# Delta net with an order of its own for each engine and the last join's products in turn; S5 kernel products in four column groups

## The reference, cut to what matters

```python
# gated DeltaNet: 4 heads x 128, forward and backward, chunked
decay = jnp.where(tril, jnp.exp(jnp.where(tril, diff, 0.0)), 0.0)
a_mat = jnp.where(strict, jnp.einsum('bhnid,bhnjd->bhnij', kb, k) * decay, 0.0)
sys = jnp.eye(DN_CHUNK, dtype=q.dtype) + a_mat
sol = lax.linalg.triangular_solve(sys, rhs, left_side=True, lower=True, unit_diagonal=True)
attn = jnp.where(tril, jnp.einsum('bhnid,bhnjd->bhnij', q, k) * decay, 0.0)
def step(state, inp):
    v_new = u_i - jnp.einsum('bhck,bhkv->bhcv', w_i, state)
    o_i = jnp.einsum('bhck,bhkv->bhcv', q_i, state) + jnp.einsum('bhij,bhjv->bhiv', attn_i, v_new)
    state = state * jnp.exp(gl_i)[..., None, None] + jnp.einsum('bhck,bhcv->bhkv', k_i, v_new)

# S5: 32 groups x 16 channels, one 64-dim complex diagonal state per group, forward and backward
bu = jnp.einsum('blgp,gnp->blgn', u.astype(jnp.complex64), b_bar)
_, state = lax.associative_scan(_ssm_combine, (a, bu), reverse=reverse, axis=1)
y = jnp.real(jnp.einsum('blgn,gpn->blgp', state, c))
```

## Time and profile before

| | |
|---|---|
| median of 3 runs | 1445.17 us (1445.14 to 1446.3) |
| the profiled execution, its own time | 1445.08 us |
| its span in the trace | 1443.3 us, 24501 instructions |
| TensorE (PE) busy | 1324.0 us, 92% |
| VectorE (DVE) busy | 1055.1 us, 73% |
| ScalarE (ACT) busy | 859.0 us, 60% |
| GpSimd (POOL) busy | 377.0 us, 26% |
| `in_projection` | 0 to about 316 us |
| `delta_net` | about 318 to 526 us |
| the rest (S5, output projection, router, experts) | about 529 to 1443 us |

### The profile page before, as it was taken

How to read it: one execution, slowest core, us unless ns; L and a number is a source line. 1 busy time by engine, 2 the same in 40 slices (tenths; PEclk the granted TensorE clock), 3 DMA queues, 4 the chain that set the end, 5 groups by cost and what they waited for, 6 DMA issues and landing times. The chain is left out here.

```text
span 1443.3 us, 24501 instructions
## 1 busy us (share of the span) xinstructions
PE 1324.0 (92%) x8394; PEld 1116.5 (77%) x8394; DVE 1055.1 (73%) x1330; ACT 859.0 (60%) x1162; POOL 377.0 (26%) x377
## 2 busy tenths in 40 slices
PE   4999999977999879999973899999999999999994
PEld 3999888866888878668863688888888888888871
DVE  6895787674777648542127788888888888888847
ACT  7473435564656354562222588877788888777742
POOL 5020122008565637312201111111111111111130
PEclk9999999998999999999975899999999999999997
DMA  9174986411233129801114899999999999999865
GB/s 267 57 231 129 293 253 178 138 41 51 47 126 94 26 103 349 313 16 44 45 62 159 329 387 419 410 415 409 415 411 411 412 408 416 404 417 412 362 231 220
DMA packets 151607, 357.47 MB, mean 248 GB/s; under 512 B 42447, under 2 KB 97003, under 8 KB 124395
## 3 DMA queue, kind: packets, MB, share of 16 engines
q1 hardware_dynamic: 131755, 297.04, 54.8%
q0 software_dynamic: 11904, 40.42, 8.3%
q10 hardware_dynamic: 7872, 19.01, 3.3%
HBM read 287.64 MB, written 68.78 MB: 247 GB/s over the span
## 5 line engine op out<-in xcount | busy, mean ns | idle before, releaser
L2820 PE MATMUL gate_up_mm<-w_hi,gathered_T_hi 128*128 128x512 f32 x528 | 212.9, 403 | 7.8 <-DVE gathered_T_lo L3003 7.8
L2822 PE MATMUL gate_up_mm<-w_hi,gathered_T_lo 128*128 128x512 f32 x528 | 208.0, 394 | 0.0
L2821 PE MATMUL gate_up_mm<-w_lo,gathered_T_hi 128*128 128x512 f32 x528 | 207.5, 393 | 0.0
L2998 DVE TENSOR_TENSOR w_lo<-w_down,w_hi 128x2048 fp32r<-128x2048 f32 x66 | 148.5, 2289 | 51.9 <-ACT w_hi L2926 51.9
L2998 DVE TENSOR_TENSOR w_lo<-w_gate,w_hi 128x2048 fp32r<-128x2048 f32 x66 | 150.8, 2289 | 20.6 <-ACT w_hi L2926 19.7
L2926 ACT ACTIVATE w_hi<-w_gate 128x2048 fp32r<-128x2048 f32 x66 | 126.9, 1923 | 54.0 <-PE gate_up_mm L2822 32.2
L2926 ACT ACTIVATE w_hi<-w_up 128x2048 fp32r<-128x2048 f32 x66 | 126.7, 1922 | 49.9 <-PE down_mm L2857 49.9
L2998 DVE TENSOR_TENSOR w_lo<-w_up,w_hi 128x2048 fp32r<-128x2048 f32 x66 | 150.8, 2287 | 4.4
L2926 ACT ACTIVATE w_hi<-w_down 128x2048 fp32r<-128x2048 f32 x66 | 125.0, 1918 | 37.5 <-issue 17.9
L2771 POOL COPY gather_idx<-slot_token 128x1 int32 (+1 forms) x34 | 21.8, 640 | 477.1 <-PE x_turned L2810 450.3
L2820 PEld LDWEIGHTS gate_up_mm<-w_hi,gathered_T_hi 128*128 128x128 f32 x528 | 100.7, 191 | 33.6 <-issue 11.4
(11 more groups left out here) (506 smaller groups left out, 3063.2 us busy)
## 6 DMA issues: line engine op xcount, KB each, us to landing
w_down<-in_expert_w_down SPq DMA_DIRECT2D x66, 1024.0 KB, 7.2
w_gate<-in_expert_w_gate SPq DMA_DIRECT2D x64, 1024.0 KB, 7.5
w_up<-in_expert_w_up SPq DMA_DIRECT2D x64, 1024.0 KB, 8.3
expert_rows_dram<-ones SPq DMA_DIRECT2D x32, 512.0 KB, 6.3
expert_rows_dram<-expert_out ACTq DMA_DIRECT2D x32, 512.0 KB, 8.6
x<-s_rows_dram SPq DMA_DIRECT2D x9, 1184.0 KB, 6.9
s_rows<-s_rows_dram SPq DMA_DIRECT2D x7, 1184.0 KB, 8.1
w_raw<-in_w_in SPq DMA_DIRECT2D x12, 512.0 KB, 5.4
```

The source lines that it names most:

```text
L2820: pe.matmul(dst, xT_hi[:, k, :], hi[:, at, cols], start=k == 0, stop=False)
L2821: pe.matmul(dst, xT_hi[:, k, :], lo[:, at, cols], start=False, stop=False)
L2822: mm = pe.matmul(dst, xT_lo[:, k, :], hi[:, at, cols], start=False, stop=k == KT - 1)
L2998: dve.tensor_tensor(lo[:, at, :], flat(j), hi[:, at, :].bitcast(F32), ALU.subtract).then_inc(S["piece_lo"], 1)
```

## The change

Three parts.

1. `delta_schedule` takes the engine's name and yields from a table `STEP_ORDER` with a row for each of PE, DVE, ACT and GpSimd; an entry names operation, direction and chunk. So one engine's order no longer follows another's. ACT's `vdec` becomes an operation of its own: it reads `vnew` from SBUF, not V from PSUM, and PE waits for it before `new_state`, no longer before `attend`.
2. `z6` and `d6` are one entry for both directions, and their products alternate head by head between forward and backward.
3. The S5 kernel's 8 pairs of a call go to four groups of 32 output columns (partitions 0 to 127), in turn, and 2 pairs to each. The copies of ACT and DVE cover 128 partitions and a quarter of the columns. `store_M` issues 64 DMAs of a quarter of the size for each half, where there were 16.

```diff
+STEP_ORDER = {
+    "PE": "z4 f 0, z4 b 0, read_k f -1, read_k b -1, d4 f 0, d4 b 0, read_q f -1, read_q b -1, turn4 f 0, turn4 b 0, "
+          "solve f -1, solve b -1, z5 f 0, z5 b 0, attend f -1, attend b -1, d5 f 0, d5 b 0, kq f 1, kq b 1, "
+          "turn5 f 0, turn5 b 0, new_state f -1, new_state b -1, z6 f 0, kk f 2, kk b 2, d6 f 0",
+    "DVE": "read_k f -1, d4 f 0, read_k b -1, d4 b 0, base f 1, attend f -1, attend b -1, d5 f 0, d5 b 0, kq f 1, "
+           "kq b 1, new_state f -1, new_state b -1, kk f 2, kk b 2",
+    "ACT": "z4 f 0, z4 b 0, read_q f -1, turn4 f 0, turn4 b 0, solve f -1, solve b -1, z5 f 0, z5 b 0, read_q b -1, "
+           "vdec f -1, vdec b -1, turn5 f 0, turn5 b 0, decay f 2, z6 f 0, z6 b 0, decay b 2, d6 f 0, d6 b 0",
...
+}
-    steps = [("decay", 0), ("kk", 0), ("decay", 1), ("spread_tt", 0), ("alev4", 0), ("spread_t", 0), ("alev5", 0),
-             ("mask", 0), ("kk", 1), ("kq", 0)]
     for t in range(TT + 1):
-        steps += [("z4", t), ("alev4", t + 1), ("read_k", t - 1), ("vb", t), ("d4", t), ("base", t + 1),
-                  ("turn4", t), ("read_q", t - 1), ("z5", t), ("solve", t - 1), ("decay", t + 2), ("d5", t),
-                  ("attend", t - 1), ("mask", t + 1), ("alev5", t + 1), ("turn5", t), ("add_o", t - 1),
-                  ("new_state", t - 1), ("z6", t), ("kk", t + 2), ("kq", t + 1), ("d6", t),
-                  ("spread_tt", t + 1), ("spread_t", t + 1)]
...
                 elif name == "z6":
-                    wait("t_out", d, 2 * t + 2)
-                    wait("amat", d, t + 1)
-                    lo, up = late(d), early(d)
+                    for way in range(2):
+                        wait("t_out", way, 2 * t + 2)
+                        wait("amat", way, t + 1)
                     for h in range(H):
-                        mm = pe.matmul(X[d][up, h, 0:64], ab_b[d][lo, b, h, up], tt_b[d][lo, b, h, lo],
-                                       start=True, stop=True)
-                    mm.then_inc(S["z"][d], 1)
+                        for way in range(2):
+                            lo, up = late(way), early(way)
+                            mm = pe.matmul(X[way][up, h, 0:64], ab_b[way][lo, b, h, up], tt_b[way][lo, b, h, lo],
+                                           start=True, stop=True)
+                            if h == H - 1:
+                                mm.then_inc(S["z"][way], 1)
...
                 elif name == "attend":
-                    wait("vdec", d, t + 1)
                     wait("vn", d, t + 1)
...
                 elif name == "new_state":
+                    wait("vdec", d, t + 1)
                     wait("o_part", d, t + 1)
...
+                elif name == "vdec":
+                    wait("vn", d, t + 1)
                     wait("kv", d, t)
                     for h in range(H):
-                        ins = act.activation(vd_b[d][:, 0, h, :], V[d][:, h, :], ACT.Copy,
+                        ins = act.activation(vd_b[d][:, 0, h, :], vn_b[d][:, 0, h, :], ACT.Copy,
                                              scale=head_col("kdec", t, d, h))
...
             for t in range(T5):
-                for h in range(2):
-                    dst = self.dram[self.HJ * hf:self.HJ * (hf + 1), t * GC:(t + 1) * GC,
+                for ch in range(8):
+                    c, h = ch // 2, ch % 2
+                    dst = self.dram[self.HJ * hf + c:self.HJ * (hf + 1):4, t * GC:(t + 1) * GC,
                                     S5_M + P * h:S5_M + P * (h + 1)].rearrange("j p n -> p j n")
...
-        for j in range(self.HJ):
+        for x in range(2):
             for ri in range(2):
-                mm = pe.matmul(self.kps[:, j * P:(j + 1) * P], self.BD[:, ri, j, :],
-                               self.g_pair(u)[ri][:, j, d:d + T5, :].rearrange("p k q -> p (k q)"),
-                               start=ri == 0, stop=ri == 1)
+                for n in range(4):
+                    j = 4 * x + n
+                    mm = pe.matmul(self.kps[2 * GC * n:2 * GC * (n + 1), x * P:(x + 1) * P], self.BD[:, ri, j, :],
+                                   self.g_pair(u)[ri][:, j, d:d + T5, :].rearrange("p k q -> p (k q)"),
+                                   start=ri == 0, stop=ri == 1)
```

More of the change, by code:

```diff
@@ L1241, in _ @@
                 dve.memset(tt_b[d][:], 0.0).then_inc(S["cleared"][d], 1)
-            for name, t, d in delta_schedule():
+            for name, t, d in delta_schedule("DVE"):
                 ch, b = chunk(t, d), t % 2
@@ L1311, in _ @@
             act.activation(tmp_b[0][:, 0, 0, 0:1], c["ones"][:, 0:1], ACT.Exp)
-            for name, t, d in delta_schedule():
+            for name, t, d in delta_schedule("ACT"):
                 b, up = t % 2, early(d)
@@ L1380, in expand @@
                 return pool.tensor_tensor(dst[d][:, 0].rearrange("p h (b c) -> p h b c", c=16), cells, mask, ALU.mult)
-            for name, t, d in delta_schedule():
+            for name, t, d in delta_schedule("POOL"):
                 ch = chunk(t, d)
```

62 lines of the change are left out of this document (35 added, 27 removed), and 2 rows, old and new, of the table STEP_ORDER.

## The result

The changed kernel took 1438.19 us, median of five runs (1436.63 to 1439.3), against 1445.81 for the kernel before (1445.14 to 1449.26): ratio 0.9937, 95% interval 0.9926 to 0.9949. It is faster by 7.6 us where 20.2 were forecast, and the time lies outside the range. The profiled execution took 1439.3 us, its span 1437.6. A later series on another chip gave 0.9945 (0.9929 to 0.9961).

What follows compares the result with a forecast made beforehand. The prediction took PE to bound both the projection and `delta_net`, with DVE close behind in the latter. 9.0 us from the S5 products plus 11.2 from `delta_net` gave 20.2 off 1445.08: 1424.9 us, range 1418.0 to 1432.0.

Steps and rivals of the forecast that it cites:

- the walk through a steady step: PE and DVE in a `delta_net` step, operation by operation: the new step takes 22.7 us against 23.57.
- the wait before `kq`: In each steady `delta_net` step PE newly waits 1.6 us for DVE, whose `o` behind `base` frees bank V.
- the 0.6 us taken off for DVE: In the projection, 0.6 us off the 9.6 saved by four calls, as later savings meet DVE without idle time.
- S5 products: Four `multiply` calls on PE in the projection fall from 3.61 to 1.2 us each: 9.0 us saved in all.
- The rival of two groups: In the S5 calls at most two column groups overlap: 6.2 us saved instead of 9, 1427.7 us; chance 0.25.
- The pairs: `z6` and `d6` in `delta_net`, both directions in turn, take 0.54 us each: 0.82 us saved per step.
- So the saving of the pairs passes through: In `delta_net` the 0.82 us per step from `z6` and `d6` shortens the step, PE bounding it.
- the 2.6 us of step 4: The `delta_net` step of 25.19 us saves 2.6, as ACT's `decay` now stands behind the `turn5` copies.
- DVE binds the step: Rival: late blocks delay `base`, the wait before `kq` is 2.6 us, six steps save nothing: 1430.9 us; chance 0.13.
- step 0: First step of `delta_net`: saves its pairs and the wait before `turn4`, 0.82 + 1.26 = 2.1 us.
- the tail: End of `delta_net`: pairs, `turn4` wait and the last `attend`'s wait for `vdec` save 0.82 + 1.0 + 1.1 = 2.9 us.
- GpSimd's queue: Rival: `store_M`'s small DMAs cost c us each; from c = 0.86 the 20 us are gone, at 1.0 1465; chance 0.02.

Runs made afterwards that it cites:

- pairs_only: The kernel before with only `z6` and `d6` taking both directions in turn, all old orders kept: ratio 1.0004 to the kernel before.
- pairs_turn5: pairs_only with ACT's copies of `turn5` moved ahead of `decay`: ratio 0.9943 to the kernel before.
- mask_late: middle_early with GpSimd's masks held back until DVE's `base` is done: ratio 0.9895 to the kernel before.
- filled11: middle_early with 11 products of the identity before each `kq` f from the second step on: ratio 0.9941 to the kernel before.
- middle_early: The changed kernel with DVE's two additions of the first `kernel_middle` moved from j = 1 to the end of j = 0: ratio 0.9941 to the kernel before.

## Why the prediction was right or wrong

The step that failed is the walk through a steady step, in its term for the wait before `kq`: 1.6 us in the sum, 2.57 measured, because the new order puts GpSimd's masks beside DVE's `base` and the two hold each other up. With it came a cost that the sum did not have at all, the slower clock behind that wait. A second, smaller failure lies in the S5 part, in the 0.6 us taken off for DVE.

**S5 products, 9.0 us forecast, 6.0 as built.** The call: 1.2 forecast, 1.0 measured. The rival of two groups had 2.06 us to come out and is refuted: two records on the same columns don't hold up the neighbour's first. `store_M` cost 65.1 us / 128 = 0.51 a DMA (0.5 forecast) and nobody waited for it. What failed is "I take off 0.6" for DVE. The earlier trace rows showed idle time of DVE ahead of j = 2; I took it for room, but the third call needs what DVE does behind the convolution, a reduction and a weight split of j = 1. There DVE was only 3.4 us early, in a row without idle time, and the two faster calls before it take 5.2. So PE arrives first, and the wait of 2.3 to 2.7 us with the slower clock behind it takes back 2.6 us (8.6 with the repair, 6.0 without).

**The pairs, 0.82 a step.** They gave 0.68, at 0.61 us each where I said 0.54. "So the saving of the pairs passes through" was argued from PE's busy row. It is false in the old order: pairs_only gives nothing, for ACT's copy of `turn5` b was just in time. It passes only with ACT's new order, a part of the change on which my sum put no more than the 2.6 us of step 4. That step was right (25.19 to 22.72 in pairs_turn5).

**The wait before `kq`, 1.6 forecast, 2.57 measured.** This is the term that was mis-sized. The place, the releaser and the reason (`o` behind `base` on bank V) were right, and so was the walk: with the masks behind `base` the wait is 1.57 and the step 22.60, against 1.6 and 22.7, as long as `base` isn't late. What I left out is POOL's place in it: I took `base`'s 7.2 us from a step in which POOL was idle, and did not look at what POOL does beside it in the new order. The rival *DVE binds the step* had 2.6 us and 23.57 to come out, which is what happened at full clock, but its reason, late blocks, isn't what sets the 2.57: with the overlap `kq` waits as long wherever between 6.6 and 7.4 us `base` begins. Late blocks alone cost 0.3 to 0.8 us in three steps of mask_late. That the number fits is in part luck, and its time, 1430.9, is still 7 us too low.

**The clock.** Nothing in my sum had it. In steps 1 to 6 the changed kernel's trace has 148.9 us where 6 x 23.59 = 141.5 would be the steps at full clock; of the extra 7.4 us, 4.5 are `kq` products of 2.71, 3.52, 2.96 and 3.43 us behind the wait instead of 2.02, and 1.5 are waits for POOL's `TT`; the rest I have not separated. How much the clock costs in the time of the whole kernel stays open, as filled11 kept it at 1.00 up to 480 us and measured no faster than middle_early.

**Where the forecast held.** The waits before `turn4` went; step 0 saved 2.3 (2.1 forecast); the tail saved 5.4 (2.9 forecast, so the rest is luck: the old tail also waited 0.54 us for POOL's `TT`, and its `read_k` took 3.2 us instead of 2.0 at a granted clock of 0.50); `attend` no longer waits for `vdec`.

**In the sum**: by the means of the traces 3.0 us are missing in the S5 part, and 10.8 in `delta_net`. There steps 1 to 6 miss 12.7 (6.2 saved forecast, 6.5 lost): 5.3 because a plain step takes 23.59 and not 22.7, and the 7.4 above. The tail and step 0 give 2.6 more than forecast, and 0.8 is lost ahead of the first `z4`. The 13.8 us stand beside 12.6 by the medians. One figure of a rival is off: GpSimd's queue would have taken the 20 us from about c = 0.85 on, not 0.86; nothing hangs on it, as c was 0.51.

## What to carry to other kernels

A wait that a change adds must be sized with everything that runs beside the releaser in the new order, GpSimd first: an operation's duration holds only for the neighbours it was measured with. When two uses are fused into one in-order entry, the fused one needs the later of their inputs, so look at which engine makes it and what stands ahead of it there. And the busiest engine's saving passes through only if the next engine is early: ask the trace by how much, for each thing that the engine takes over.

## What the runs showed of the hardware

- f32 products of 128x32 weights and 128 columns on four column groups in turn start 32 ns apart (1.01 us for 32 records), against 113 on one group.
- DVE's two-operand instructions and copies in SBUF and GpSimd's `tensor_tensor` exclude each other for whole instructions: 64x8 elements took 0.78 us instead of 0.16. Reductions kept their 0.68 us, and two products with an operand in PSUM their 1.29.
- After PE had stood for 2.6 us or more, `kq` ran slower behind the wait, at the 1.2 GHz level for part or all of it, in 21 of 36 steps, and at 2.4 GHz in the others, which makes a step 23.59 or up to about 25.2 us. It also did so behind waits of 1.33, 1.64 and 1.89 us.
- A GpSimd DMA of 32 pieces took 0.51 us of its queue, one of 128 pieces 0.55.
